# Conditioning weights: twelve of the attention stage's twenty units multiplied by VectorE, with TensorE left to sum over partitions

## The reference, cut to what matters

```
c_act = jax.nn.silu(c)                      # 1 x 1024
for i in range(DEPTH):                      # two layers
    mod = c_act @ ada_w[i] + ada_b[i]       # ada_w[i]: 1024 x 6144
    sh_m, sc_m, gt_m, sh_f, sc_f, gt_f = jnp.split(mod, 6, axis=-1)
    h = modulate(rmsnorm(x, norm_mix_g[i]), sh_m, sc_m)
    y = fox_attention(h, ...)               # layer 0: 16 heads
    x = x + gt_m[:, None, :] * y
    ...                                     # the experts use sh_f, sc_f, gt_f
```

## Time and profile before

| what | value |
|---|---|
| median of three runs | 2057.15 us (2052.92 to 2060.86) |
| profiled execution, its own time | 2052.83 us |
| its span, first to last instruction | 2051.0 us |
| mean granted TensorE clock | 0.918 |
| TensorE matrix products busy | 1677.1 us (82%) |
| VectorE busy | 686.2 us (33%) |
| HBM read | 578.88 MB, 283 GB/s over the span |
| `ada_w` DMAs | 24 of 2048 KB |

### The profile page before, as it was taken

The page is one execution under the profiler, slowest core; times in us unless marked ns, Lnnn a source line. Parts: engine busy times, 40 slices in busy tenths (PEclk is TensorE's granted clock), DMA queues, the critical chain, the costliest instruction groups (busy, mean ns, idle before and its releaser), DMA issues.

```text
span 2051.0 us, 25313 instructions
## 1 busy us (share of the span) xinstructions
PE 1677.1 (82%) x10192; PEld 995.6 (49%) x10193; DVE 686.2 (33%) x1441; ACT 258.1 (13%) x630; POOL 93.2 (5%) x125
## 2 busy tenths in 40 slices
PE   5999987866666578886666657989999999999998
PEld 3655553322212236332221223775997486769963
DVE  1213463111101116521010112883566333344672
ACT  1002121000000012100000001223111022221100
POOL 1001001000000000750000000000000000000000
PEclk9999999988878789998787878999999999999999
DMA  9969349999999995999999999204345282404351
GB/s 362 406 241 364 164 167 417 413 421 422 422 422 422 421 413 217 415 421 406 422 422 422 422 414 387 93 1 164 117 163 197 89 297 90 156 11 164 124 205 41
DMA packets 122679, 581.31 MB, mean 283 GB/s; under 512 B 10820, under 2 KB 15272, under 8 KB 67160
## 3 DMA queue, kind: packets, MB, share of 16 engines
q1 hardware_dynamic: 120416, 573.92, 69.9%
q10 hardware_dynamic: 1064, 3.17, 0.4%
q0 software_dynamic: 1104, 2.86, 0.4%
HBM read 578.88 MB, written 1.05 MB: 283 GB/s over the span
## 4 chain that ended last, share of the span: by engine, by line
PE 42%; DMA 31%; PEld 12%; DVE 7%; issue 4%; ACT 2%; SPq 1%; DVEq 1%; PEldq 1%; ACTq 0%
DMA ring_buffer<-in_exp_w 29%; PEld ps L2075 10%; PE ps L1379 7%; PE ps L2104 6%; PE ps L2792 4%; PE ps L1404 4%; PE ps L750 3%; PE ps L1904 3%; PE ps L506 2%; PEld ps L2046 2%; PE ps L913 1%; PE ps L763 1%; PE ps L2783 1%; SPq L1264 1%; DMA ring_buffer<-in_ada_w 1%
## 5 line engine op out<-in xcount | busy, mean ns | idle before, releaser
L1379 PE MATMUL ps<-ring_buffer,arena 128*32 128x512 f32 x2008 | 303.5, 754 | 170.5 <-DMA ring_buffer<-in_exp_w 167.6
L1379 PEld LDWEIGHTS ps<-ring_buffer,arena 128*32 128x32 f32 x2008 | 78.7, 134 | 376.2 <-issue 283.9
L1404 PE MATMUL ps<-ring_buffer,arena 128*32 128x512 f32 x1088 | 153.2, 715 | 93.2 <-DMA ring_buffer<-in_exp_w 81.0
L1575 DVE TENSOR_TENSOR arena<-arena,ps 128x512 f32<-128x512 f32 x18 | 19.1, 1063 | 406.5 <-PE ps L1379 406.5
L2075 PE MATMUL ps<-arena,ring_buffer 128*128 128x128 f32 x1152 | 133.9, 276 | 3.8 <-issue 3.8
L1404 PEld LDWEIGHTS ps<-ring_buffer,arena 128*32 128x32 f32 x1088 | 40.3, 128 | 194.8 <-issue 184.7
L2075 PEld LDWEIGHTS ps<-arena,ring_buffer 128*128 128x128 f32 x1152 | 130.8, 192 | 5.8 <-issue 5.8
L2104 PE MATMUL ps<-ring_buffer,arena 128*128 128x512 f32 x252 | 111.0, 594 | 3.8 <-issue 2.0
L2075 PE MATMUL ps<-hT,ring_buffer 128*128 128x128 f32 x864 | 99.4, 275 | 0.0
L2075 PEld LDWEIGHTS ps<-hT,ring_buffer 128*128 128x128 f32 x864 | 97.9, 192 | 0.0
L1339 PEld LDWEIGHTS ps<-arena,xn 128*128 128x128 f32 x640 | 73.9, 193 | 14.3 <-issue 14.0
(11 more groups left out here) (558 smaller groups left out, 2047.6 us busy)
## 6 DMA issues: line engine op xcount, KB each, us to landing
ring_buffer<-in_exp_w SPq DMA_DIRECT2D x379, 1024.0 KB, 18.7
ring_buffer<-in_ffn_w SPq DMA_DIRECT2D x30, 2048.0 KB, 11.6
ring_buffer<-in_ada_w SPq DMA_DIRECT2D x24, 2048.0 KB, 12.6
ring_buffer<-in_c_w_in SPq DMA_DIRECT2D x8, 2048.0 KB, 13.5
ring_buffer<-in_attn_w_in SPq DMA_DIRECT2D x6, 2048.0 KB, 16.5
ring_buffer<-in_ab_w_in SPq DMA_DIRECT2D x3, 2048.0 KB, 19.0
ring_buffer<-in_ffn_w SPq DMA_DIRECT2D x6, 1024.0 KB, 5.5
arena<-in_exp_w SPq DMA_DIRECT2D x5, 1024.0 KB, 9.0
```

Source lines behind the costliest of these rows:

```text
L1379: ins = pe.matmul(ps[c, bank, :], tokens[:, 4 * phase + k, c], halves[j][:, k, :], start=(phase == 0 and k == 0), stop=(phase == 1 and k = ...
L1404: ins = pe.matmul(ps[c, bank, :], tokens[:, 2 * phase + k, c], halves[j][:, k, half * 512:(half + 1) * 512], start=(phase == 0 and k == 0) ...
```

## The change

Twelve of the twenty conditioning units that these stages hold go to VectorE: the thirds 1 and 2 of layer 0 (8 units) and the third 0 of layer 1 (4 units). The other eight (layer 1, thirds 1 and 2) stay on TensorE in the heads, now in the steps 4 to 11.

- `condition_dve` waits for the unit's landing and runs four instructions on 128x1024 elements: weights of one block k and one half of the columns, times the column of c that belongs to the block, added to an accumulator of 128x2048. In the first pair's block k = 0 there is nothing to add to, and it is a TENSOR_SCALAR; otherwise a SCALAR_TENSOR_TENSOR. The last of the four counts up `condition_taken`.
- The accumulators are two tiles that are free at that time: `xn` (128x2048) for third 1 of layer 0 and later third 0 of layer 1, `gates` for third 2 of layer 0.
- `condition_rows_summed` sums an accumulator over the partitions on TensorE with 4 matrix products; the stationary operand `spread_one` is a 128x32 window with one column of ones. It is called three times: behind piece 2, behind piece 4, and in the heads' step 12.
- Ten units are multiplied in the projections, behind the tiles 1, 3, 5, 7, 9, 11, 13, 16, 17 and 19 (`UNIT_AFTER`); unit 8, the ninth, first waits for the sum that frees `xn`. The eleventh goes into the heads' steps 0 to 3, a quarter each, the twelfth into steps 4 and 5, a half each, in both cases ahead of VectorE's wait for the step's scores.
- Behind the pieces c = 0 to 5 stand now 2, 2, 2, 1, 2, 0 conditioning units in the ring (`AFTER`), three behind `attn_f`, then the eight of TensorE. SyncE waits for `condition_taken` where the slot was held by a unit of VectorE's. `release` counts the units of VectorE that follow as used too.
- `condition_rows` moves from tile 15 to tile 18, `condition_turn` from behind piece 4 to behind piece 5, and `condition_finish` to behind the forget gates' three instructions, at the stage's end.
- Some semaphores of other stages are merged, with the same waits.

```diff
+        def condition_dve(dve, layer, third, pair, acc, parts=PARTS):
+            v = chain["dve"]
+            n = next(n for n in ring.by_dve if ring.units[n][0] == ("ada", layer, third, pair))
+            dve.wait_ge(weights_landed[ring.slots[n]], ring.landed_at[n])
+            w = ring.view(n, 2, 2048)
+            for k, half in parts:
+                c, cs = col("c", 2 * pair + k), slice(1024 * half, 1024 * half + 1024)
+                if pair == k == 0:
+                    ins = dve.tensor_scalar(acc[:, cs], w[:, k, cs], c, None, ALU.mult)
+                else:
+                    ins = dve.scalar_tensor_tensor(out=acc[:, cs], in0=w[:, k, cs], scalar=c, in1=acc[:, cs],
+                                                   op0=ALU.mult, op1=ALU.add)
+                if (k, half) != (1, 1):
+                    v(ins)
+                else:
+                    ins.then_inc(condition_taken, 1)
+                    dve.wait_ge(condition_taken, ring.by_dve.index(n) + 1)
+
+        def condition_rows_summed(pe, taken, third, acc, first, last):
+            pe.wait_ge(condition_taken, taken)
+            for n in range(4):
+                row = WIDE - 1 - (4 * third + n)
+                pe.matmul(ps[n * WIDE:(n + 1) * WIDE, COND, :], spread_one[:, row:row + WIDE],
+                          acc[:, 512 * n:512 * (n + 1)], start=first, stop=last, skip_group_check=True)
+            pe.drain().then_inc(acc_summed, 1)
...
                 for n in range(first, last):
                     _, source, k, m = ring.units[n]
-                    if ring.free_at[n]:
+                    if ring.free_at[n] - 1 in ring.by_dve:
+                        sp.wait_ge(condition_taken, ring.by_dve.index(ring.free_at[n] - 1) + 1)
+                    elif ring.free_at[n]:
                         sp.wait_ge(weights_used, ring.free_at[n])
...
+            BY_DVE = [(0, third, pair) for third in (1, 2) for pair in range(4)] + [(1, 0, pair) for pair in range(4)]
+            AFTER = (2, 2, 2, 1, 2, 0)
...
-                    release(pe)
-                    for n in range(2 * c, 2 * c + 2):
-                        condition(pe, 0, 1 + n // 4, n % 4, n == 0, n == 7)
-                condition_summed(pe)
+                    release(pe, 1 + AFTER[c])
+                    if c == 2:
+                        condition_rows_summed(pe, 4, 1, acc[0], True, False)
...
                     if c == 4:
+                        condition_rows_summed(pe, 8, 2, acc[1], False, True)
+                        condition_summed(pe)
+                    else:
                         condition_turn(pe, 2, 4, 12)
...
+                    if n in UNIT_AFTER:
+                        m = UNIT_AFTER.index(n)
+                        if m == 8:
+                            dve.wait_ge(acc_summed, 1)
+                        condition_dve(dve, *BY_DVE[m], acc[BY_DVE[m][1] == 2])
...
+                condition_finish(dve, 2, 0, 4, 12)
+            UNIT_AFTER = (1, 3, 5, 7, 9, 11, 13, 16, 17, 19)
...
-                    if i < 12:
-                        condition(pe, 1, i // 4, i % 4, i == 0, i == 11)
+                    if 4 <= i < 12:
+                        condition(pe, 1, i // 4, i % 4, i == 4, False)
                     if i == 12:
+                        condition_rows_summed(pe, 12, 0, acc[0], False, True)
                         condition_summed(pe)
...
+                        if i < 4:
+                            condition_dve(dve, *BY_DVE[10], acc[0], PARTS[i:i + 1])
+                        elif i < 6:
+                            condition_dve(dve, *BY_DVE[11], acc[0], PARTS[2 * i - 8:2 * i - 6])
```

More of the change, by code:

```diff
@@ L141, in take @@
     def take(self, pe, key):
+        while self.next in self.by_dve:
+            self.next += 1
         n = self.next
@@ L219, in build_program @@
         stage_done = sem("stage_done")
+        condition_taken = sem("condition_taken")
         dve_step, pool_step = sem("dve_step"), sem("pool_step")
@@ L238, in run_stages, with release @@
                 eng.drain().then_inc(stage_done, 1)
-        def release(pe):
-            pe.drain().then_inc(weights_used, 1)
+        def release(pe, units=1):
+            pe.drain().then_inc(weights_used, units)
         def stream_units(first, last):
@@ L333, in s5_parameters @@
             b_tmp = take(S_PAIRS, S_GROUP)
-            (s5_loaded, s5_wide_loaded, dt_ready, args_ready, sc_ready, par_ready, par_turned, wide_ready, wide_turned) = (
-                sem("s5_" + n) for n in ("loaded", "wide_loaded", "dt_ready", "args_ready", "sc_ready", "par_ready", "par_turned",
-                                         "wide_ready", "wide_turned"))
+            (s5_loaded, s5_wide_loaded, dt_ready, args_ready, sc_ready, par_ready, wide_ready, turned) = (
+                sem("s5_" + n) for n in ("loaded", "wide_loaded", "dt_ready", "args_ready", "sc_ready", "par_ready",
+                                         "wide_ready", "turned"))
+            PAR_TURNED, WIDE_TURNED = 1, 2
             R = S_PAIRS
@@ L509, in condition, with add_condition_dve @@
             release(pe)
+        spread_one = arena[:, 15008:15008 + 2 * WIDE]
+        def add_condition_dve(layer, third, pair):
+            ring.by_dve.append(len(ring.units))
+            add_condition(layer, third, pair)
+        PARTS = ((0, 0), (0, 1), (1, 0), (1, 1))
+        def condition_dve(dve, layer, third, pair, acc, parts=PARTS):
[22 more added lines that the diff above has]
+            pe.drain().then_inc(acc_summed, 1)
+        acc_summed = sem("acc_summed")
         def condition_summed(pe):
@@ L707, in attention @@
             n0 = len(ring.units)
+            BY_DVE = [(0, third, pair) for third in (1, 2) for pair in range(4)] + [(1, 0, pair) for pair in range(4)]
+            AFTER = (2, 2, 2, 1, 2, 0)
+            queue = iter(BY_DVE)
             for c in range(6):
                 ring.add(("attn_in", c), columns(w_in, 512 * c, 512), KD, 512)
-                if c < 4:
-                    for n in range(2):
-                        third, pair = divmod(2 * c + n, 4)
-                        add_condition(0, third + 1, pair)
+                for _ in range(AFTER[c]):
+                    add_condition_dve(*next(queue))
             ring.add(("attn_f",), columns(w_in, 3 * D, N_HEADS), KD, N_HEADS)
-            for n in range(12):
+            for unit in queue:
+                add_condition_dve(*unit)
+            for n in range(4, 12):
                 add_condition(1, *divmod(n, 4))
+            acc = [xn.rearrange("p t d -> p (t d)"), gates.rearrange("p t d -> p (t d)")]
             for c in range(2):
@@ L775, in proj_pe @@
                 ins.then_inc(p_ready, 1)
-                release(pe)
+                release(pe, 1 + len(BY_DVE) - sum(AFTER))
             def take_projection(eng, n, copy):
```

30 lines of the change are left out of this document (16 added, 14 removed).

## The result

The changed kernel takes 2043.05 us (median of six runs, 2042.07 to 2047.59); the kernel before, timed beside it, 2058.67 us (2052.92 to 2061.08). The ratio is 0.9937, 95% interval 0.9923 to 0.9952: 15.6 us by the medians, where 17.6 were forecast. In a second comparison, on another chip, it was 2045.61 against 2053.97, ratio 0.9966 (0.9954 to 0.9978). So the gain is real and its size is uncertain: 8 and 16 us by the medians, 4.5 to 16 us by the two intervals.

What follows compares the result with a forecast made beforehand. TensorE was taken to carry projections and heads almost alone. 11.1 us won in the projections plus 6.5 in the heads make 17.6, so the median goes from 2057.15 to 2039.5 us; likeliest 2035 to 2044, whole range 2031 to 2049.

Steps and rivals of the forecast that it cites:

- The projections' work and the DMA's pace: Projections: eight units leave TensorE, new waits for DMA of 1.4 and 1.2 us; 11.1 us won after VectorE's finish.
- VectorE's part: Projections: a unit costs VectorE 5.25 us, it keeps up with little cover, and its finish adds 0.6 us at the end.
- The pace of the steps by VectorE: Heads, steps 0 to 3: without units on TensorE, VectorE sets the pace at 1.94 + 1.31 = 3.25 us.
- Rival C: Projections and heads: VectorE's instruction on a ring slot takes 2.6 us, kernel slower by some 24 us, 2081; chance 0.04.
- The clock: Behind the turn: TensorE's low clock costs the forget gates 1.57 us; up to 3 us worse if it runs on.
- the 11.2 us: Heads: step 4 starts 11.2 us after step 0, 7.8 us earlier than before; 6.5 us won after the third sum.
- rival B: Clock stays low: heads' steps 0 to 3 lose 8.8 us, two projection waits 3.2; 5.6 us won, 2051.6; chance 0.09.
- B's 3.2 us: Projections: each of the two waits, before pieces 1 and 2, costs 1.6 us through the low clock.
- The row that was to speak against B: Profile of the kernel before: clock 1.00 from 234 to 238 us with TensorE busy only 2.61 of 4 us.
- The later stages: Experts' stages: their stream waits for TensorE, so the whole 17.6 us gained ahead arrives as a shift of the end.

Runs made afterwards that it cites:

- idle products in step 0: The change plus one conditioning unit's worth of idle wide products on TensorE in the heads' step 0: 2046.13 us, ratio 0.9950 to the kernel before.
- projections alone: The change with only layer 0's eight units on VectorE, the heads keeping twelve on TensorE: 2045.15 us, ratio 0.9957 to the kernel before.
- idle products in steps 0 to 3: The change plus a conditioning unit's worth of idle wide products on TensorE in each of these heads' steps: 2052.38 us, ratio 0.9980 to the kernel before.

## Why the forecast was right in the sum and wrong in a step

**The projections' work and the DMA's pace: right.** The pieces 1 and 3 began 1.2 and 1.1 us later than forecast, released by the DMA as said. The waits were 3.7 us where the forecast had 2.7 (1.4, 1.2 and 0.1): piece 1 alone waited 2.1. That the ring's order was what made them wait is shown by moving one unit: it brings 3.9 us at least at the mark.

**VectorE's part: right.** 5.24 us a unit, the unit that the second sum needs done at 115.0 and the sum begun at 116.1 (113.9 and 114.9 forecast), 0.6 us of finish at the stage's end (141.7 to 142.3). The pace of the steps by VectorE, 3.25 us, appeared in one step where the clock was up (idle products in step 0). Rival C, the slow instruction, is out: the median is 1.284 us, though single ones in the first steps of the heads took up to 1.62.

**The clock: the step that failed.** The forecast charged the low clock behind the turn with 1.57 us in the forget gates and nothing behind them. It cost 2.8 us in the gates' products (6.51 against 3.73), 1.3 in the gates' stage (8.6 against 6.7, less the finish of 0.6 that was charged), 5.3 in the steps 0 to 4 (16.5 against 11.2) and 2.8 in step 4 (7.5 against 4.7). These are some 12 us, 10.5 beyond the term, of the 11.7 us by which the mark's 5.9 fall short of 17.6; the rest is mostly that the pieces came later. The idle products in step 0 show that it is the clock and not the steps' waits: the same work of VectorE stands in the same steps. They also bear out the 11.2 us: 13.4 less the 2.9 of the group itself are 10.5, an estimate from that trace.

This was rival B, priced at 5.6 us won, to which the forecast gave 0.09. That 5.9 came at the mark is close by luck: B's 3.2 us behind the waits of pieces 1 and 2 did not come (both pieces took 14.08 us, as before), while the gates' products and stage lost 2.5 us more than the forecast's term, which B left out; the steps 0 to 4 with the unit in step 4 lost 8.1 where B had 8.8. Its mechanism was not quite the one named: not the waits between the products but, as far as is shown, the lack of wide ones. From 168 to 172 TensorE is busy all the time at 0.50, though work at half the clock also fills gaps that it would leave at the full one; and the same steps, with their gaps, ran at 1.00 once idle products stood in step 0. The row that was to speak against B was read for the wrong thing: at 234 to 238 the clock was up from the steps before and stayed, as in that experiment. Whether it comes up is another question, and rows of before had the answer: 0.66 from 152 to 156, then 0.77 and 0.80, and 1.00 only behind the first unit of the heads, which begins at 159.6:

```profile
156.00:160.00 4.00, 3.47 (x18) 2.24 (x20) 0.72 (x2) 0.09 (x1) 2.83 (x5) 0.77 0.64 268
160.00:164.00 4.00, 3.88 (x24) 1.50 (x16) 0.50 (x3) 2.09 (x5) 3.54 (x6) 0.80 0.21 31
164.00:168.00 4.00, 3.89 (x29) 2.01 (x28) 1.34 (x6) 0.81 (x4) 3.23 (x5) 1.00 0.91 373
```

The sentence of the Trainium skill (TensorE: Matmul & The Clock Gate, "HAM oscillation — how this bites in real kernels") pointed at the right loss. Its rule, waits for data between short bursts, is not all that the traces show here: the forget gates lost 2.8 us with no wait ahead of or in them, at 0.50 with TensorE busy for 4.00 of 4 us.

**The later stages: not a plain shift.** The change's two traces lie 8.6 and 10.3 us below the first trace of before with 5.9 and 6.9 at the mark. A pause of all engines (last section), 4.5 us shorter in both, is more than the rest of 2.7 and 3.4; some 1.2 to 1.6 us are lost again behind it. The pause is not all that varies there: the two traces of before differ by some 3.5 us behind the mark with pauses equal within 0.5 us each. It may also be why one and the same change was 15.6 us below before by the medians of one comparison and 8.4 by the other: only the profiled execution of each has a trace. Which part of these belongs to the change could not be settled with twelve runs or fewer of a kernel.

## What to carry to other kernels

Before taking wide products off TensorE, look at what keeps its clock up at that place: the granted clock in the windows around, and what stands there between narrow products. Work taken from where the clock would then stay low can cost more than it saves; the same work taken a few steps later, with TensorE's units in the first steps, started the output projection 9.5 to 10.6 us earlier still. And judge such a change at marks in the trace behind which nothing differs, not by the end alone, and at two of them: the stretch between shows how much the clock makes of the same work (55.9 to 59.2 us here).

## What the runs showed of the hardware that was not expected

**Extra products can bring forward what follows.** 16 idle instructions in step 0 brought the mark from 290.0 and 291.0 in the two traces of the change to 284.7, 64 of them to 287.2. The times of whole runs don't show a gain over the change: 0.9950 and 0.9980 against 0.9937 and 0.9966. The kernel before already holds idle products elsewhere, such as the ten instructions of `keep_busy` (L259) ahead of the mark; its heads' first steps hold none, and the conditioning units stood in that place.

**The engines pause in the experts' stages for a time that jumps.** Behind a loop over passes that have nothing to do, all engines go on with the last pass. TensorE's first product there shows how long it had been idle, with nothing in the profile that it waited for. The timelines at that place, first of the kernel before (layer 0, layer 1), then of the change (the same), then of the projections alone (layer 0):

```profile
714.95 0.66 PE L1390 MATMUL ps<-consts,arena 128*128 128x128 f32 x2 [12.63 <-issue]
...
1223.27 0.66 PE L1390 MATMUL ps<-consts,arena 128*128 128x128 f32 x2 [12.44 <-issue]
```

```profile
709.59 0.66 PE L1453 MATMUL ps<-consts,arena 128*128 128x128 f32 x2 [12.62 <-issue]
...
1213.05 0.66 PE L1453 MATMUL ps<-consts,arena 128*128 128x128 f32 x2 [7.93 <-issue]
```

```profile
716.68 0.66 PE L1448 MATMUL ps<-consts,arena 128*128 128x128 f32 x2 [22.32 <-issue]
```

Over the thirteen traces the pause was 12.4 to 13.1 us in layer 0, but 22.3 and 22.2 in two (projections alone, idle products in steps 0 to 3), and in layer 1 12.2 to 12.5 in eight and 7.8 to 7.9 in five. In the two long ones the DMAs of the experts' weights stop for about 10 us as well, which takes the gain of these kernels in their profiled executions: spans of 2052.4 and 2051.6 against 2051.0 and 2054.1 of the kernel before. The profile shows one thing that goes with it: its queue of the kind "instruction" moved 2 packets in the last 26 us ahead of that product in the eleven other traces and 5 in the two long ones. The rows of before and of the projections alone, both from 694 to 717 us (packets, MB, share):

```profile
q8 instruction: 2, 0.03, 0.6%
```

```profile
q8 instruction: 5, 0.08, 1.5%
```

Whether the engines wait for these packets is not shown, and what makes the pause long is open; one trace of a kernel can't tell whether it goes with the code or with the execution. It is as large as the effect under study, so times of this kernel that differ by less than 10 us need the trace beside them.
